# Causal masks moved from TensorE to VectorE, and part of the softmax weighing from VectorE to ScalarE, in two attention mixers of a long fp32 kernel

## The reference, cut to what matters

```python
s_f = einsum(q_f, k_f) * scale + cf[..., :, None] - cum_f[..., None, :]   # gated: forget gates
p_f = softmax(where(causal, s_f, -inf));   o_f = p_f @ v_f
s_d = einsum(q_d, k_d) * scale                                            # two maps
p_d = softmax(where(causal, s_d, -inf))
a_d = p_d[:, :, 0] - lam * p_d[:, :, 1];   o_d = a_d @ v_d
o_d = rmsnorm(o_d, subln) * (1 - lambda_init)
out = concatenate([o_f, o_d]) @ w_out
```

## Time and profile before

| what | us |
|---|---|
| median of 3 runs | 2626.52 (2625.72 to 2629.01) |
| the profiled execution's own time | 2627.89 |
| its span, first to last instruction | 2626.1 |
| busy, PE / DVE / ACT / POOL | 2610.0 / 1419.7 / 1023.2 / 227.6 |
| granted TensorE clock | 0.999 |

### The profile page before, as it was taken

How to read it: one execution, slowest core, us unless ns; L and a number is a source line. 1 busy time by engine, 2 the same in 40 slices (tenths; PEclk the granted TensorE clock), 3 DMA queues, 4 the chain that set the end, 5 groups by cost and what they waited for, 6 DMA issues and landing times.

```text
span 2626.1 us, 33116 instructions
## 1 busy us (share of the span) xinstructions
PE 2610.0 (99%) x12382; PEld 2131.5 (81%) x12382; DVE 1419.7 (54%) x1861; ACT 1023.2 (39%) x1588; POOL 227.6 (9%) x164
## 2 busy tenths in 40 slices
PE   8999999999999999999999999999999999999999
PEld 7888888878888888888887778888887888888777
DVE  5444248875444235444258765444236657845773
ACT  4222135654222233222145653223135553334663
POOL 0000024101000010000033111000000000012220
PEclk9999999999999999999999999999999999999999
DMA  4222233113222223222232112222222222322221
GB/s 164 96 96 96 96 104 97 65 41 105 96 96 98 99 90 102 98 97 96 96 111 82 58 64 96 96 96 96 96 88 81 78 83 85 109 93 93 84 70 56
DMA packets 70323, 239.13 MB, mean 91 GB/s; under 512 B 8528, under 2 KB 10832, under 8 KB 70224
## 3 DMA queue, kind: packets, MB, share of 16 engines
q1 hardware_dynamic: 69792, 236.91, 27.1%
q10 hardware_dynamic: 432, 0.87, 0.1%
HBM read 230.15 MB, written 2.10 MB: 88 GB/s over the span
## 4 chain that ended last, share of the span: by engine, by line
PE 92%; DVE 3%; issue 2%; ACT 1%; DVEq 0%; POOL 0%; DMA 0%; POOLq 0%; ACTq 0%; SPq 0%
PE bank L410 21%; PE bank L412 20%; PE bank L411 20%; PE score L411 5%; PE score L410 5%; PE score L412 5%; PE flip_bank L410 2%; PE flip_bank L411 2%; PE flip_bank L412 2%; PE score L1140 1%; PE flip_bank L1168 1%; PE bank L2697 1%; PE score L2665 1%; PE score L1857 1%; PE bank L1190 1%
## 5 line engine op out<-in xcount | busy, mean ns | idle before, releaser
L393 DVE TENSOR_TENSOR w_lo<-w_raw,w_hi 128x1024 fp32r<-128x1024 f32 x427 | 525.8, 1233 | 537.3 <-ACT w_hi L353 526.5
L410 PE MATMUL bank<-h_hi,w_hi 128*128 128x512 f32 x1856 | 740.5, 399 | 1.1 <-DVE w_lo L393 1.1
L412 PE MATMUL bank<-h_hi,w_lo 128*128 128x512 f32 x1856 | 724.4, 390 | 0.0
L411 PE MATMUL bank<-h_lo,w_hi 128*128 128x512 f32 x1856 | 723.3, 390 | 0.0
L353 ACT ACTIVATE w_hi<-w_raw 128x1024 fp32r<-128x1024 f32 x427 | 447.8, 1051 | 396.3 <-DMA w_raw<-stream 396.0
L410 PEld LDWEIGHTS bank<-h_hi,w_hi 128*128 128x128 f32 x1856 | 349.1, 188 | 75.8 <-issue 5.0
L412 PEld LDWEIGHTS bank<-h_hi,w_lo 128*128 128x128 f32 x1856 | 348.8, 188 | 73.7
L411 PEld LDWEIGHTS bank<-h_lo,w_hi 128*128 128x128 f32 x1856 | 349.4, 188 | 71.8 <-issue 2.4
L539 ACT ACTIVATE hid_hi<-tmp 128x512 f32 (+1 forms) x88 | 55.6, 632 | 409.7 <-DVE tmp L753 409.7
L747 DVE TENSOR_TENSOR tmp<-bank,rstd 128x512 f32<-128x512 f32 x132 | 91.1, 691 | 147.2 <-PE bank L412 146.9
L534 ACT ACTIVATE tmp<-tmp 128x512 f32<-128x512 f32 x88 | 55.6, 632 | 247.7 <-DVE tmp L747 247.7
(11 more groups left out here) (516 smaller groups left out, 3819.5 us busy)
## 6 DMA issues: line engine op xcount, KB each, us to landing
w_raw<-stream SPq DMA_DIRECT2D x427, 512.0 KB, 3.2
tmp<-tmp SPq DMA_DIRECT2D x64, 64.0 KB, 2.1
x_tok<-x SPq DMA_DIRECT2D x4, 512.0 KB, 6.7
wx_raw<-stream SPq DMA_DIRECT2D x4, 512.0 KB, 4.7
out<-out_tok SPq DMA_DIRECT2D x8, 256.0 KB, 2.0
tmp<-qr SPq DMA_DIRECT2D x16, 64.0 KB, 2.7
tab_in_f<-tables SPq DMA_DIRECT2D x1, 704.0 KB, 10.4
cos_sin<-rope ACTq DMA_DIRECT2D x1, 512.0 KB, 5.0
```

The costliest lines, as they stand in the source:

```text
L393: nc.vector.tensor_tensor(w_lo[:, s, :], w_raw[:, s, :], w_hi[:, s, :].bitcast(F32), ALU.subtract).then_inc(lo_ready, 1)
L410: nc.tensor.matmul(dst, whi, xhi, start=start, stop=False)
L411: nc.tensor.matmul(dst, whi, xlo, start=False, stop=False)
L412: return nc.tensor.matmul(dst, wlo, xhi, start=False, stop=stop)
```

## The change

The mask matmuls go. VectorE adds the same bf16 table in place to the diagonal 128x128 block of each score tile before it takes the maximum: at b = 0 to four blocks (those of b = 0 and b = 1), at b = 2 and 3 to two, at b = 1 to none. A `drain` stands between the addition and the maximum.

`weigh` is cut up. `invert` takes the reciprocal in its old place, and for difference heads multiplies the second one by lambda (one column). `scale_probs` on ScalarE then multiplies the probabilities: both slots for gated heads (this ends the weighing), the second map for difference heads. VectorE's remaining instruction for difference heads, p0 * scalar - p1, moves down in its step behind the rotary additions and waits for ScalarE. Two semaphores are new, `inverted` and `scaled`.

```diff
+                def scale_probs(k):                      # ScalarE
+                    g, b = STEPS[k]
+                    act.wait_ge(inverted, NSTEP * layer + k + 1)
+                    for c in (1,) if is_diff(g) else (0, 1):
+                        p = probs[:, k % 2, c, 0:P * (b + 1)]
+                        ins = nc.scalar.activation(p, p, ACT.Copy, scale=softstat[:, 2 * k + c, 2:3])
+                    ins.then_inc(scaled if is_diff(g) else weighed, 1)
...
                     for kind, h in units_at(k, "qk"):
                         if not is_diff(h):
                             high_half(kind, h)
+                    if k < NSTEP:
+                        scale_probs(k)
...
                 def maxima(k):                           # VectorE
+                    b = STEPS[k][1]
                     dve.wait_ge(scored, NSTEP * layer + k + 1)
+                    if b == 0:
+                        diagonal = score[:, :, :].rearrange("p c (t n) -> p c t n", n=2 * P)[:, :, :, 0:P]
+                        causal = table_b("causal").unsqueeze(1).unsqueeze(1).broadcast_to([P, 2, 2, P])
+                    else:
+                        diagonal = score[:, :, P * b:P * b + P]
+                        causal = table_b("causal").unsqueeze(1).broadcast_to([P, 2, P])
+                    if b != 1:
+                        nc.vector.tensor_tensor(diagonal, diagonal, causal, ALU.add)
+                        dve.drain()
                     nc.vector.tensor_reduce(...)
...
                 def weigh(k):
-                    dve.wait_ge(exped, NSTEP * layer + k + 1)
-                    nc.vector.reciprocal(softstat[:, 2 * k:2 * k + 2, 2], softstat[:, 2 * k:2 * k + 2, 1])
-                    dve.drain()
                     p0, p1 = probs[:, k % 2, 0, 0:width], probs[:, k % 2, 1, 0:width]
-                    if is_diff(g):
-                        nc.vector.tensor_scalar(p1, p1, softstat[:, 2 * k + 1, 2:3], lam[:, 4 + layer:5 + layer], ...)
-                        dve.drain()
-                        nc.vector.scalar_tensor_tensor(out=p0, in0=p0, scalar=softstat[:, 2 * k, 2:3], in1=p1, ...)
-                    else:
-                        nc.vector.tensor_scalar(p0, p0, softstat[:, 2 * k, 2:3], None, ALU.mult)
-                        nc.vector.tensor_scalar(p1, p1, softstat[:, 2 * k + 1, 2:3], None, ALU.mult).then_inc(weighed, 1)
+                    dve.wait_ge(scaled, TB * DIFF_HEADS * layer + k + 1)
+                    nc.vector.scalar_tensor_tensor(out=p0, in0=p0, scalar=softstat[:, 2 * k, 2:3], in1=p1, ...)
+
+                def invert(k):
+                    dve.wait_ge(exped, NSTEP * layer + k + 1)
+                    ins = nc.vector.reciprocal(softstat[:, 2 * k:2 * k + 2, 2], softstat[:, 2 * k:2 * k + 2, 1])
+                    if is_diff(STEPS[k][0]):
+                        dve.drain()
+                        ins = nc.vector.tensor_tensor(softstat[:, 2 * k + 1, 2:3], softstat[:, 2 * k + 1, 2:3],
+                                                      lam[:, 4 + layer:5 + layer], ALU.mult)
+                    ins.then_inc(inverted, 1)
...
                     if k < NSTEP:
-                        weigh(k)
+                        invert(k)
...
+                    if k < NSTEP and is_diff(g):         # behind v_low and rope_add
+                        weigh(k)
...
                 def scores(k):                           # TensorE
-                    for c in range(2):
-                        for e in blocks:
-                            end = score_cols(e).stop
-                            ins = nc.tensor.matmul(score[:, c, end - P:end], table_b("identity"), table_b("causal"),
-                                                   start=False, stop=is_diff(g) and e == blocks[-1])
```

More of the change, by code:

```diff
@@ L250, in build @@
         scored, maxed, exped = sem("scored"), sem("maxed"), sem("exped")
+        inverted, scaled = sem("inverted"), sem("scaled")
         weighed, flipped, flip_half, flip_out = (sem(n) for n in ("weighed", "flipped", "flip_half", "flip_out"))
@@ L850, in weigh @@
                     width = P * (b + 1)
-                    dve.wait_ge(exped, NSTEP * layer + k + 1)
-                    nc.vector.reciprocal(softstat[:, 2 * k:2 * k + 2, 2], softstat[:, 2 * k:2 * k + 2, 1])
-                    dve.drain()
-                    p0, p1 = probs[:, k % 2, 0, 0:width], probs[:, k % 2, 1, 0:width]
-                    if is_diff(g):
-                        nc.vector.tensor_scalar(p1, p1, softstat[:, 2 * k + 1, 2:3], lam[:, 4 + layer:5 + layer],
-                                                ALU.mult, ALU.mult)
-                        dve.drain()
-                        nc.vector.scalar_tensor_tensor(out=p0, in0=p0, scalar=softstat[:, 2 * k, 2:3], in1=p1,
-                                                       op0=ALU.mult, op1=ALU.subtract).then_inc(weighed, 1)
-                    else:
-                        nc.vector.tensor_scalar(p0, p0, softstat[:, 2 * k, 2:3], None, ALU.mult)
-                        nc.vector.tensor_scalar(p1, p1, softstat[:, 2 * k + 1, 2:3], None, ALU.mult).then_inc(weighed, 1)
+                    p0, p1 = probs[:, k % 2, 0, 0:width], probs[:, k % 2, 1, 0:width]
+                    dve.wait_ge(scaled, TB * DIFF_HEADS * layer + k + 1)
+                    nc.vector.scalar_tensor_tensor(out=p0, in0=p0, scalar=softstat[:, 2 * k, 2:3], in1=p1,
+                                                   op0=ALU.mult, op1=ALU.subtract).then_inc(weighed, 1)
+                def invert(k):
+                    dve.wait_ge(exped, NSTEP * layer + k + 1)
+                    ins = nc.vector.reciprocal(softstat[:, 2 * k:2 * k + 2, 2], softstat[:, 2 * k:2 * k + 2, 1])
+                    if is_diff(STEPS[k][0]):
+                        dve.drain()
+                        ins = nc.vector.tensor_tensor(softstat[:, 2 * k + 1, 2:3], softstat[:, 2 * k + 1, 2:3],
+                                                      lam[:, 4 + layer:5 + layer], ALU.mult)
+                    ins.then_inc(inverted, 1)
                 def flip_low(k):
@@ L1139, in scores @@
                                 rows = slice(HEAD * c, HEAD * c + HEAD)
-                                nc.tensor.matmul(score[:, c, score_cols(e)], q[rows, g % 2, P * e:P * e + P],
-                                                 kk[rows, g % 2, 0:P * (e + 1)],
-                                                 start=q is q_hi and kk is k_hi and e == blocks[0], stop=False)
-                    for c in range(2):
-                        for e in blocks:
-                            end = score_cols(e).stop
-                            ins = nc.tensor.matmul(score[:, c, end - P:end], table_b("identity"), table_b("causal"),
-                                                   start=False, stop=is_diff(g) and e == blocks[-1])
+                                ins = nc.tensor.matmul(score[:, c, score_cols(e)], q[rows, g % 2, P * e:P * e + P],
+                                                       kk[rows, g % 2, 0:P * (e + 1)],
+                                                       start=q is q_hi and kk is k_hi and e == blocks[0],
+                                                       stop=is_diff(g) and q is q_lo and e == blocks[-1])
                     if not is_diff(g):
```

## The result

The changed kernel takes 2641.33 us (median of 6 runs, 2640.13 to 2643.89) against 2626.57 us: 14.8 us more, ratio 1.0055, 95% interval 1.0045 to 1.0066. The forecast was 2632, with 2641.0 as the upper end of the range. The sign was right, the size a third of what came; the time is that of the second rival, the clogged queues. The execution that was profiled is the slowest of the six (2643.89 us).

A forecast was written before the change was run, and what follows sets the result against it. The kernel was taken to be bound by the sum of TensorE's instructions. Per layer, 5.9 us of new waits against 3.4 saved made it 5 us slower in both layers: 2632 us median, 8-in-10 range 2620 to 2641.

The forecast's parts named there:

- second rival: VectorE's delays in one head reach the next: (A) 1.7 each, (B) 1.5, (C) 3, (D) 1.2 us; 2641, chance 0.2.
- TensorE's saving: 64 mask matmuls per layer go from TensorE: 3.4 us per layer, 6.7 us in both, bounds 4 and 9.
- (A): Passage b = 2 to b = 3 of difference heads 1 to 3: late maximum stalls TensorE 0.9 us each, 2.7 per layer.
- step 12: A smaller stall of the same kind as (B), put at 0.2 us.
- (B): Step 16, first gated pair, b = 0: scalings ahead of ScalarE's table load delay it; TensorE loses 0.65 us.
- the ring: One PSUM score set ties TensorE, VectorE and ScalarE: next scores wait for exponentials, these for the maximum; 0.54 us spare at step 15.
- The product held by GpSimd: VectorE's one-column product by lambda, with two SBUF inputs, waits until GpSimd's instruction ends: over 1 us where GpSimd works.
- (C): Steps 20 to 24, where TensorE already waits: later exponentials and masks saved without gain, 1.75 us per layer, bounds 0.3 and 3.
- (D): Step 30 loses 0.4 us by the mask, step 31's transposition 0.2 waiting for two scalings; bounds 0.2 and 1.2.

The follow-up runs named there:

- the load: Kernel before without any mask; VectorE instead reduces SBUF columns for the mask's time, in front of the maximum (2632.6 us) or directly behind it (2629.1 us).
- light GpSimd: GpSimd's rotary products cut to 16 of 512 columns: on the kernel before 2626.1 us, with the masks also on VectorE 2627.1 us.
- masks only: Kernel before with the masks added by VectorE, the weighing left on VectorE as before: 2635.2 us, ratio 1.003.
- weighing only: Kernel before with the changed weighing (inverse, scaling on ScalarE, late last weighing), masks left on TensorE: 2634.0 us, ratio 1.0025.
- changed, low part first: Changed kernel with VectorE's low part of the transposed probabilities moved in front of mask and maximum: 2655.0 us, ratio 1.0107.

## Why the prediction was wrong, point by point

**TensorE's saving** (6.7 us, bounds 4 to 9): right. 5.4 measured (2.6 to 7.9), and the shift at step 4 is -0.37 in the first layer, four pairs at 0.09 as worked out.

**(A), with step 12 and (B)** (2.7 + 0.85 = 3.55 us of waits per layer): the step that failed. From step 6 to 18 the shift grows by 7.29 and 5.45 us, and some 1.0 saved has been eaten as well: 8.3 and 6.5, of which about 1.7 in the first layer belongs to the clock (below). So about 6.5 per layer, almost twice the term. By the table of shifts, the stretches with the three places that (A) priced (7 to 8, 11 to 12, 12 to 16) grow by 1.8, 1.5 and 1.1 us in the first layer, where the 1.5 is the clock's, and by 1.0, 0.8 and 1.3 in the second, against 0.9 each; but 1.7 and 1.4 us more are lost from step 8 to 11, which it priced at nothing. The last stall, at step 17, is where (B) put it, 1.10 us at 509.90 instead of 0.65.

The mechanism named was there and is shown (the scaling in front of the squares: 2634.0 to 2625.9 when it is moved), but it is only half of the loss. Three things were missing. In the difference heads the masks were counted only as the last link of the chain of (A); but the masks alone make 13.2 us of difference, and in the difference heads their time counts even where nothing in the ring waits for it: of the load, 12 times 0.5 to 0.75 us or some 7 us per layer by the prediction's own prices, 4.2 came out in the first layer's shift behind the maximum (+3.43 at step 16 against -0.79 without a mask). VectorE has hardly any room there, and the room is taken by GpSimd, which holds its work for 7.9 of the 66.6 us of steps 4 to 15; of this hold the prediction priced one instruction, as a delay in a chain, and not the room that it takes (the pair with light GpSimd: 1.0 us instead of 7.9). And TensorE meets the lateness at the transposition, before the scores; except in (B) I had measured the spare time only at the scores.

**The product held by GpSimd**: right as a fact (1.0 to 1.1 us at steps 4, 9 and 14, 0.16 where GpSimd rests) and wrong as a cause, since taking the product away changes nothing. The trace of that kernel shows the next instruction held in its place, 1.69 us for one of 0.65. The rule quoted from the Trainium skill, "SBUF — State Buffer", section "Who interferes with whom", is borne out for a one-column instruction and also for a scan (2.21 against 1.21 us).

**(C)** (1.75 us per layer): measured 0.6 of shift from step 18 to 24 plus 0.7 of eaten saving, 1.3 in both layers. The waits are where they were forecast, 1.33 and 0.83 us against 0.31 and 0.68 in the earlier trace rows, grown to about 2 together as said: right, a little high.

**(D)** (0.6 per layer): 0.40 at step 31 as forecast, but 0.79 at the last transposition, where 0.2 was put, and 0.42 at step 28 for `k_lo`, which was not seen: 1.6. The scaling at 0.61 to 0.72 us for the wide steps instead of 0.48 to 0.63 is part of that.

**The rivals.** The second one had the right place, and was given 0.2. It said that VectorE must no longer catch up at b = 1; the light GpSimd shows that just this decides. Its (A) and (B), 6.6 us, are what came; that the whole sum, 14.8, is the measured number is luck: per layer its (C) was 1.7 us too high and its (D) 0.4 too low, and the saving 1.3 too high in both together. Its reason, that GpSimd is pushed later by more two-input work in its time, holds for the scaling's part alone; with the masks the hold is no longer than before. The signs for it stood in the profile before: in the third difference head, steps 8 to 11, VectorE was busy 21.29 of 22.40 us (third number behind the comma), which the 74% of the whole mixers in the earlier trace rows hid.

```profile
448.12:470.52 22.40, 22.40 (x128) 18.05 (x127) 21.29 (x31) 12.81 (x31) 11.30 (x6) 1.00 0.28 81
```

**What stays open.** The profiled execution after is 16.0 us longer than the one before. The shifts of the two layers give 14.0 of it; 0.9 lie between the last scores of the first layer and the first of the second, where the last transposition waits 0.79; 1.1 lie ahead of both mixers, where the code is the same (first scores at 407.80 against 406.71 us); behind the last scores of the second layer the two take the same time, as the 0.77 us that the last transposition waits there are made good later. Why the masks cost 2.6 us more in the medians than the load that stands for them stays open. So does how the masks' 13.2 us divide between hold, queue and ring in a kernel that has all three.

## What to carry to other kernels

Moving work from the full engine to one that is 74% busy is worth only what the worst stretch has room for: look at the busy share by head or by step, and look in it for instructions that another engine makes longer. An instruction put in the middle of an in-order queue costs its wait to everything behind it; here the same scaling cost 8 us more in one place than at the end of the same step. And the wait that a profile names first may be a symptom: reordering for it made the two kernels 6.5 and 12.5 us slower.

## What the runs showed of the hardware that was not expected

TensorE's clock fell to its lower level inside the mixers once there was waiting. After, first layer, steps 10 and 11 (first fence: timeline of PE; second: the stretch from 469 to 477 us, busy times, then the granted clock, 0.79 on the mean):

```profile
468.56 0.51 PE L1164 MATMUL score<-k_hi,q_hi 64*128 64x512 f32 x2 [0.57 <-ACT probs L602]
...
470.90 0.63 PE L412 MATMUL bank<-h_lo,w_hi 128*128 128x512 f32 x1
471.32 0.63 PE L413 MATMUL bank<-h_hi,w_lo 128*128 128x512 f32 x1
```

```profile
469.00:477.00 8.00, 8.00 (x40) 6.08 (x37) 6.81 (x15) 5.61 (x11) 1.29 (x1) 0.79 0.15 45
```

Matmuls start 0.43 us apart instead of 0.23, at 1.2 instead of 2.4 GHz, for 3.4 us, which costs 1.7 us. It follows waits of 1.14 and 0.57 us. The mixers of the kernel before had none of this, and the second layer of the changed one had none either in the execution that was profiled. Of the other kernels, the four with the most waiting had it in their mixers, the rest, masks only and weighing only among them, did not. The slowest experiment (changed, low part first) had 17 us of it in its mixers, so that about 8.5 us of its 27 are the clock's; one such stretch:

```profile
1433.00:1443.00 10.00, 8.61 (x34) 7.02 (x35) 6.03 (x13) 5.92 (x15) 0.51 (x1) 0.66 0.12 30
```

A wait of TensorE can thus cost more than its length; that the waits bring the clock down is read from what goes before it, and no run tests it by itself. A wait of 1.44 us at 449.82 was not followed by a lower clock, so its length alone does not tell. Outside the mixers the kernel before has such a stretch too, 3.4 us from 2437.8 us on; nine of the eighteen profiled executions have it and nine have not, in code that is the same. Two traces can differ by 1.7 us for that alone.
